# Expert tokens in a mixture-of-experts stage: picked by products, or fetched by row and transposed

## The reference

```
def _swiglu(h, wg, wu, wd):
    return (jax.nn.silu(h @ wg) * (h @ wu)) @ wd

probs = jax.nn.softmax((hf @ router).astype(F32), axis=-1)
top_p, top_i = lax.top_k(probs, TOP_K)
top_p = top_p / jnp.sum(top_p, -1, keepdims=True)
gates = jnp.sum(jax.nn.one_hot(top_i, N_EXPERTS) * top_p[..., None], axis=1)
for e in range(N_EXPERTS):
    out = out + gates[:, e:e + 1] * _swiglu(hf, wg[e], wu[e], wd[e])
```

## Time and profile before

| | us |
|---|---|
| median of 3 runs | 3322.02 |
| lowest, highest | 3319.12, 3328.23 |
| the profiled execution | 3326.0 |
| its span, first to last instruction | 3324.2 |
| PE busy in that span | 2939.2 |
| DVE, ACT, POOL busy | 1619.3, 1080.2, 98.6 |

### The profile page before, as it was taken

How to read it: one execution, slowest core, us unless ns; L and a number is a source line. 1 busy time by engine, 2 the same in 40 slices (tenths; PEclk the granted TensorE clock), 3 DMA queues, 4 the chain that set the end, 5 groups by cost and what they waited for, 6 DMA issues and landing times. The chain is left out here.

```text
span 3324.2 us, 42033 instructions
## 1 busy us (share of the span) xinstructions
PE 2939.2 (88%) x16604; PEld 2571.2 (77%) x16604; DVE 1619.3 (49%) x2073; ACT 1080.2 (32%) x1405; POOL 98.6 (3%) x92
## 2 busy tenths in 40 slices
PE   7999778999699997689999999959999685679997
PEld 6889677878578896679999999948888564668786
DVE  3536643232434466366666777663332337442333
ACT  2334113222232432045444555442222323232221
POOL 0012100000000220000000000000000000000000
PEclk9999889999899998789999999979999896889998
DMA  4210025151322001067666766643341210151521
GB/s 146 83 44 1 4 74 147 47 138 48 98 70 76 16 1 51 23 179 205 181 182 179 204 176 188 186 118 84 89 116 35 81 30 2 58 136 51 143 57 64
DMA packets 438966, 316.87 MB, mean 95 GB/s; under 512 B 22576, under 2 KB 395312, under 8 KB 438704
## 3 DMA queue, kind: packets, MB, share of 16 engines
q1 hardware_dynamic: 438832, 314.96, 33.2%
HBM read 312.29 MB, written 2.62 MB: 95 GB/s over the span
## 5 line engine op out<-in xcount | busy, mean ns | idle before, releaser
L1425 PE MATMUL psum<-x_split,gate_up_split 128*128 128x512 f32 x1056 | 416.2, 394 | 38.5 <-DVE gate_up_split L1501 30.5
L1426 PE MATMUL psum<-x_split,gate_up_split 128*128 128x512 f32 x1056 | 414.9, 393 | 0.0
L1427 PE MATMUL psum<-x_split,gate_up_split 128*128 128x512 f32 x1056 | 414.9, 393 | 0.0
L2406 PE MATMUL psum<-x_slots_split,gate_up_split 128*128 128x320 f32 x1424 | 377.4, 342 | 7.5 <-DVE gate_up_split L2550 5.6
L1710 PE MATMUL psum<-w_split,x_split 128*128 128x256 f32 (+1 forms) x2400 | 298.6, 287 | 32.6 <-DVE w_split L1744 26.0
L1710 PEld LDWEIGHTS psum<-w_split,x_split 128*128 128x128 f32 x2400 | 294.3, 195 | 37.9 <-ACT w_split L1724 26.7
L1710 PE MATMUL psum<-x_split,w_split 128*128 128x512 f32 x1248 | 297.4, 398 | 25.2 <-DVE w_split L1744 19.9
L2407 PE MATMUL psum<-x_slots_split,gate_up_split 128*128 128x160 f32 x1424 | 314.7, 241 | 0.0
L1523 DVE TENSOR_TENSOR arena<-arena,psum 128x512 f32<-128x512 f32 x66 | 45.4, 688 | 530.6 <-ACT arena L1484 530.6
L1710 PEld LDWEIGHTS psum<-x_split,w_split 128*128 128x128 f32 x1248 | 237.3, 192 | 85.8 <-ACT w_split L1724 22.2
L2406 PEld LDWEIGHTS psum<-x_slots_split,gate_up_split 128*128 128x128 f32 x1424 | 261.6, 189 | 13.7 <-ACT gate_up_split L2491 5.8
(11 more groups left out here) (411 smaller groups left out, 4501.9 us busy)
## 6 DMA issues: line engine op xcount, KB each, us to landing
arena<-in_moe_w_gate SPq DMA_DIRECT2D x91, 512.0 KB, 4.3
arena<-in_moe_w_up SPq DMA_DIRECT2D x91, 512.0 KB, 5.7
arena<-in_moe_w_down SPq DMA_DIRECT2D x176, 256.0 KB, 3.8
arena<-in_ffn_w_gu SPq DMA_DIRECT2D x88, 512.0 KB, 5.3
arena<-in_w_in SPq DMA_DIRECT2D x36, 1024.0 KB, 5.3
arena<-in_ffn_w_down SPq DMA_DIRECT2D x132, 256.0 KB, 3.6
arena<-in_ffn_w_gate SPq DMA_DIRECT2D x22, 512.0 KB, 4.2
arena<-in_ffn_w_up SPq DMA_DIRECT2D x22, 512.0 KB, 5.6
```

The costliest lines, as they stand in the source:

```text
L1425: nc.tensor.matmul(out, w[0], XR[:, 0, k, :], start=k == 0, stop=False)
L1426: nc.tensor.matmul(out, w[0], XR[:, 1, k, :], start=False, stop=False)
L1427: mm = nc.tensor.matmul(out, w[1], XR[:, 0, k, :], start=False, stop=k == DT - 1)
L2406: hi = lambda start, stop: nc.tensor.matmul(out, wt[0], XE[:, k8, :, :].rearrange("p s n -> p (s n)"), start=start, stop=stop)
```

## The change

The plain token rows are stored in DRAM (`tokens`, 512 x 1024) by one 2,048 KB transfer in `stage_router`, and SP waits for it before that stage's barrier. The split of `H` into `HR` is gone, on ACT and on DVE. A constant `token` holds the numbers 0 to 511. In `stage_moe` a new function `indices()` on PE multiplies the pick matrix by that constant, in plain float32: 4 products of one column for slots 0 to 127 and 4 for slots 128 to 159, into bank 6. DVE casts the two columns to integers (`idx`). POOL then issues two indirect transfers, which fetch row `idx[slot]` of `tokens` into partition `slot`: 128 rows into `rows` and 32 into `more`, 4 KB each. `gather()` now turns these by 16 transposes (8 of 128 x 128, 8 of 32 x 128) into the same places of banks 0 to 2. An empty slot fetches row 0, which `PT` leaves out later. For the first expert all of this stands in a row at the stage's start; in a pass, `indices()` stands at f = 7, for the next expert, and `gather()` stands where it stood. Two of the pool of semaphore names are given up (`MOST_SIGNALS` 124 to 122), and the constants get the 4 columns of `token`.

```diff
@@ -1283,6 +1283,7 @@
...
         self.rotary = nc.dram_tensor("rotary", (2, P, SEQ), F32, kind="Internal").ap()
+        self.tokens = nc.dram_tensor("tokens", (SEQ, D), F32, kind="Internal").ap()
         base = (nc.sbuf_base + 31) // 32 * 32
@@ -1307,7 +1308,6 @@
...
-        self.HR = place("x_tok_split", 2 * TT * D, XR0, F32R).rearrange("p (s t d) -> p s t d", s=2, t=TT)
         self.HIDS = place("hidden_slots_split", 2 * FU * CAP, HIDS0, F32R).rearrange("p (s f t) -> p s f t", s=2, t=CAP)
@@ -2150,12 +2150,14 @@
...
         gates = SM[:, 0:32].rearrange("p (t e) -> p t e", e=8)
-        loaded, mms, centred, exped, step = (self.sig(n) for n in ("router_loaded", "router_products", "router_centred", "router_exped", "dve_steps"))
+        loaded, mms, centred, exped, step, rows = (self.sig(n) for n in ("router_loaded", "router_products", "router_centred", "router_exped", "dve_steps", "token_rows_stored"))
         bc = lambda x: x.broadcast_to([P, TT, 8])
...
                 sp.dma_start(rw, router.rearrange("(k p) e -> p k e", p=P)).then_inc(*loaded.up(16))
+                sp.dma_start(self.tokens.rearrange("(t p) d -> p t d", p=P), self.H).then_inc(*rows.up(16))
+                sp.wait_ge(*rows.at(16))
@@ -2240,12 +2242,12 @@
...
 ...
         SVW = self.SVW
-        step, rounded, ready, mms, iota_in = (self.sig(n) for n in ("dve_steps", "feature_tile_split", "slot_inputs_ready", "slot_products", "slot_iota_loaded"))
+        step, ready, mms, iota_in = (self.sig(n) for n in ("dve_steps", "slot_inputs_ready", "slot_products", "slot_iota_loaded"))
         FAR = -4096.0
@@ -2258,7 +2260,6 @@
...
                     act.sem_inc(*self.sig("moe_" + n).up(8))
-                nc.scalar.activation(HR[:, 0], H, ACT.Copy).then_inc(*rounded.up())
@@ -2272,8 +2273,6 @@
...
                 nc.vector.tensor_tensor(tot, selc[:, TT - 1, :], sel[:, TT - 1, :], ALU.add).then_inc(*ready.up())
-                dve.wait_ge(*rounded.at(1))
-                s.link(nc.vector.tensor_tensor(HR[:, 1], H, HR[:, 0].bitcast(F32), ALU.subtract))
                 s.link(nc.vector.tensor_scalar(H, H, ALPHA, None, ALU.mult))
@@ -2304,12 +2303,15 @@
...
     def stage_moe(self, gate_w, up_w, down_w):
         GSPL, DSPL, GRAW, DRAW, SM = self.GSPL, self.DSPL, self.GRAW, self.DRAW, self.SM
...
         d_loaded = [self.sig(f"moe_down_loaded{r}") for r in range(DRING)]
+        rows, more = self.area(XR0, D), self.area(XR0 + D, D)[0:N - P, :]
+        idx = self.A[:, XR0 + 2 * D:XR0 + 2 * D + 2].bitcast(U32)
+        idx_mm, idx_ready, asked, rows_loaded = (self.sig(n) for n in ("token_index_products", "token_indices_ready", "token_rows_asked", "moe_token_rows_loaded"))
@@ -2379,12 +2381,19 @@
...
+                    ident = self.cf("ident")
                     for k, (b, o) in enumerate(XB):
+                        nc.tensor.transpose(self.bank(b)[:, o:o + P], rows[:, k * P:(k + 1) * P], ident)
+                        mm = nc.tensor.transpose(self.bank(b)[:, o + P:o + N], more[:, k * P:(k + 1) * P], ident[0:N - P, 0:N - P])
+                    mm.then_inc(gathered.sem, 1)
+
+                def indices():
+
+                    for j, (s0, n) in enumerate(((0, P), (P, N - P))):
                         for t in range(TT):
-                            for s in range(2):
-                                mm = nc.tensor.matmul(self.bank(b)[:, o:o + N], HR[:, s, t, k * P:(k + 1) * P], PSEL[:, t, :],
-                                                      start=t + s == 0, stop=t == TT - 1 and s == 1)
-                    mm.then_inc(gathered.sem, 1)
+                            mm = nc.tensor.matmul(self.bank(6)[0:n, j:j + 1], PSEL[:, t, s0:s0 + n].bitcast(F32), self.cf("token")[:, t:t + 1],
+                                                  start=t == 0, stop=t == TT - 1)
+                    mm.then_inc(idx_mm.sem, 1)
@@ -2463,9 +2472,13 @@
...
                             down(w, f - 2)
+                        if f == 7:
+                            wait(pe, w, pick_ready, 1, 2)
+                            wait(pe, w, pt_ready, 2, 1)
+                            indices()
                     down(w, FU - 2)
                     down(w, FU - 1)
-                    wait(pe, w, pick_ready, 1, 2)
+                    wait(pe, w, rows_loaded, 32, 64)
                     wait(pe, w, halves, FU, FU)
@@ -2477,9 +2490,27 @@
...
                 pe.wait_ge(pick_ready.sem, pick_ready.base + 1)
+                indices()
+                pe.wait_ge(rows_loaded.sem, rows_loaded.base + 32)
                 gather()
...
                 passes(pe, body)
+
+            @block.gpsimd
+            def _(pool):
+                def fetch():
+                    for j, x in enumerate((rows, more)):
+                        n = P if j == 0 else N - P
+                        pool.indirect_dma_start(x, None, self.tokens, bass.IndirectOffsetOnAxis(ap=idx[0:n, j:j + 1], axis=0)).then_inc(rows_loaded.sem, 16)
+
+                def body(w, e):
+                    wait(pool, w, idx_ready, 2, 4)
+                    pool.sem_inc(asked.sem, 1)
+                    fetch()
+
+                pool.wait_ge(idx_ready.sem, idx_ready.base + 2)
+                fetch()
+                passes(pool, body)
@@ -2571,6 +2602,10 @@
...
+                def indices():
+                    nc.vector.tensor_copy(idx[:, 0:1], self.bank(6)[:, 0:1]).then_inc(idx_ready.sem, 1)
+                    nc.vector.tensor_copy(idx[0:N - P, 1:2], self.bank(6)[0:N - P, 1:2]).then_inc(idx_ready.sem, 1)
+
                 def add(w, e, n):
@@ -2598,6 +2633,9 @@
...
                             pick(w + 1)
+                        if f == 7:
+                            wait(dve, w, idx_mm, 1, 2)
+                            indices()
                     split_d(w, FU)
@@ -2617,6 +2655,8 @@
...
                 pick(0)
+                dve.wait_ge(idx_mm.sem, idx_mm.base + 1)
+                indices()
                 for b in range(3):
@@ -3060,6 +3100,7 @@
...
     put("tail", (ar >= 2 * P - CAP)[:, None])
+    put("token", ar[:, None] + P * np.arange(TT)[None, :])
     ci = np.zeros((P, NCI, P), np.int32)
...
```

More of the change, by code:

```diff
@@ L65 @@
 OWN_MU = 96
-MOST_SIGNALS = 124
+MOST_SIGNALS = 122
 LASTING = ("moe_", "ffn_gate_up_loaded", "w_piece_loaded")
@@ L107 @@
 CF = {}
-for _name, _n in (("ident", 128), ("headcol", 8), ("invf", 1), ("iota8", 8), ("tail", 1)):
+for _name, _n in (("ident", 128), ("headcol", 8), ("invf", 1), ("iota8", 8), ("tail", 1), ("token", TT)):
     CF[_name] = (sum(n for _, n in CF.values()), _n)
@@ L2240, in stage_slots @@
     def stage_slots(self, ahead):
-        nc, H, HR, SM = self.nc, self.H, self.HR, self.SM
+        nc, H, SM = self.nc, self.H, self.SM
         sel, selc, tri, ones = self.area(SLOT_TMP, TT, 8), self.area(SLOT_TMP + 32, TT, 8), self.area(SLOT_TMP + 64, P), self.area(SLOT_TMP + 192, P)
@@ L2306, in stage_moe @@
     def stage_moe(self, gate_w, up_w, down_w):
-        nc, H, HR, HID, TMP, XE, PSEL, PT, YE = self.nc, self.H, self.HR, self.HIDS, self.TMP, self.XE, self.PSEL, self.PT, self.YE
+        nc, H, HID, TMP, XE, PSEL, PT, YE = self.nc, self.H, self.HIDS, self.TMP, self.XE, self.PSEL, self.PT, self.YE
         GSPL, DSPL, GRAW, DRAW, SM = self.GSPL, self.DSPL, self.GRAW, self.DRAW, self.SM
```

## The result

| | before | after |
|---|---|---|
| median, us (5 runs each) | 3319.12 | 3301.91 |
| lowest, highest | 3316.31, 3328.23 | 3299.61, 3304.53 |
| the profiled execution, its span | 3326.0, 3324.2 | 3304.53, 3302.7 |

The ratio is 0.9948, 95% interval 0.9937 to 0.9960. The kernel is 17.2 us faster, where 38 us were forecast: right in sign and inside the range, at its upper end, but with less than half of the gain. The step that failed is the price of the 16 transposes: 1.3 us a pass forecast, 3.41 us measured, and behind them a clock that falls in half of the passes. The rest of this document is about the missing 21 us.

The account below looks back on a forecast made before the run. PE's own instructions were taken to bound the expert stage. Eight passes at 4.3 us saved give -34.4 us, the stage's start -3.6, together -38.0: from 3322.0 to 3284.0 us, range 3275 to 3303.

Parts of the forecast that it names:

- What bounds the kernel: Expert stage: PE's own instructions set a pass's length, busy 732.1 of 734 us; time taken off PE counts in full.
- The removed gather: In each pass, before the second half's downs: 64 products of 0.111 us, 7.11 us, go away.
- The 16 transposes: At the gather in a pass: 8 large 0.8 us, 8 small 0.5 us, together 1.3 us, bounds 1.0 to 1.6.
- The clock: In the passes: PEclk stays 1.00 all through, as low work lasts only 1.5 us at a time.
- rival 2: In the passes: PE's clock falls to 1.2 GHz, once a pass 3303 us, twice 3322 us; chance 0.06.
- The index products: In a pass at f = 7: 16 instructions on PE's path add 1.5 us, between 1.1 and 1.8.
- The entry: Start of the expert stage, first pick through first gather: -3.6 us, bounds -7.3 to 0.
- X: Time of the first indirect fetch at the stage's start: 6.3 us assumed, between 2.6 and 9.7.
- The fetch: Indirect transfers in a pass: covered by 18.7 us before PE needs the rows, so costed at nothing.
- rival 3: Fetch in a pass comes late: gain of 38 us gone at 23.5 us, 3374 us at 30; chance 0.08.
- The store: Router stage: the 2,048 KB store of token rows hides under PE's router products and costs nothing.
- Rival 4: In a pass: 32 small products and transposes at 0.22 us take 7.0 us, only the start changes, 3318; chance 0.04.

Follow-up runs that it names:

- Grouped: Against the changed kernel, gather() issues the 8 transposes of 128 x 128 first, then the 8 of 32 x 128; 3281.61 us, ratio 0.9872 to the kernel before.
- the even kernel: Against the changed kernel, the 160 rows are split 80 and 80 in fetch, index products and 16 equal transposes; 3279.18 us, ratio 0.9864 to the kernel before.

## Why the prediction was half right

- **What bounds the kernel: right.** PE waits as before, and half of a gather taken off PE came back whole.
- **The removed gather, 7.1 us: right** (3.53 us for its half).
- **The 16 transposes, 1.3 us, bounds 1.0 to 1.6: wrong, the step that failed.** They took 3.41 us. I priced each size from 8 transposes of one size in a row and added. The rows of the order in the section on the change show the sizes in turn, and I did not ask what the turn does to the loads. The miss is 2.1 us a pass, 17 us in all. Grouped, the same 16 took 1.57 us, inside my bounds. That kernel is what I had priced: 43.0 us under the kernel before beside it, where 38.0 were forecast, with 32.7 of them in the passes by its trace, where 34.4 were.
- **The clock, "PEclk 1.00 all through": wrong in 4 of 8 passes.** It is rival 2 in part, at 1.6 us a fall where I had 2.4 for every pass, 6.3 us in all. I argued that low work lasts 1.5 us at a time; it lasted 3.41. So this follows from the first miss: in the profiled executions of the kernels with the sizes grouped or even no pass fell.
- **The index products, 1.5 us: 1.22**, which gives 2.2 us back.
- **What is left:** 7.11 - 3.41 - 1.22 = 2.48 us, against 2.3 between gathers. The trace shows where: the second down product behind the gather starts 0.33 us after the first (1500.97, 1501.30), where it was 0.27 in the kernel before (1603.98, 1604.25), and the second `gate_up` product behind the index products 0.25 us after the first (1478.14, 1478.39), where it was 0.15 (1577.59, 1577.74).
- The sum by its own steps: 34.4 - 16.9 + 2.2 - 1.4 - 6.3 = 12.0 us, against 12.3 measured.
- **The entry, -3.6 us: -2.3 measured** (-2.5 for the slot stage, +0.3 from pick to `gate_up`). X was 6.3 us as assumed; index products 1 us shorter, transposes 2.6 us longer. The estimate from the Trainium skill (DMA: Bandwidth & Descriptors, Anatomy of one DMA) was 5.5 us; the trace has 6.3. That 6.3 came out to the digit is luck: it was a point near the middle of 2.6 to 9.7.
- **The fetch: right.** From issue to landing 4.3 to 6.3 us, 18 transfers, far from the 23.5 at which rival 3 would have decided. The store: right, nothing.
- **Rival 4** named the size of the transposes (0.22 us each; 3.41 / 16 = 0.21) for a reason that the even kernel refutes, and its index products were not long (1.22 / 16 = 0.08 us).
- **A slip:** the 92.1 us between gathers before took the first by its weight load and the second by its product. From product to product they are 91.9 to 92.0, and my 4.3 us a pass would give 87.6 instead of 87.8.

## What to carry to other kernels

A price per instruction from a row of equal ones holds for a row of equal ones: before adding small matmuls or transposes, look at the order in which sizes alternate, and in the trace at whether each weight load starts ahead of its product. Sort by size, or cut the work evenly; here either gave 20 us or more for one or a few lines. A thin stretch on PE can be paid twice, in itself and in the clock: look for PEclk below 1.00 also in the busy code right after it, where the changed kernel showed it, and not in the stretch alone.

## What the runs showed of the hardware

- Transposes of 128 and 32 rows in turn: 0.43 us a pair, each load starting with its own product. The same grouped: 0.12 and 0.08 us each; 80 rows each in turn: 0.07 us each. Between 128-row products and 80-row transposes the loads ran ahead; between 128 and 32 rows they didn't.
- The clock stayed at 2.4 GHz through 4.39 us of 80-row transposes with their loads ahead, and 8.6 us of the same at 1.2 GHz didn't raise it. It fell to 1.2 GHz behind 16 transposes of 128 and 32 rows in turn (3.41 us) in 4 of 8 passes, and among 32 of them in 8 of 8, in one profiled execution each.
- Products of one or two columns: 16 plain float32 instructions 1.10 us, 8 of fp32r 0.53 us.
- POOL's issue of an indirect transfer of 128 rows took 1.11 us at the entry and 2.22 to 2.24 us in the eight passes, beside a DVE subtraction with two inputs in SBUF (1478.39 to 1480.66 in the first). That the one slows the other wasn't isolated here. The Trainium skill (SBUF — State Buffer, Who interferes with whom) states that such an instruction contends with a POOL instruction that reads SBUF; it also tells of a probe in which it did not stall transfers. It cost nothing, as the rows were not needed for 18 us.
